# Gathered tokens of a mixture-of-experts layer: 128 partitions instead of 64, and products with identity columns instead of transposes

## The chip, the cores and the metric

The kernel runs on one core of one Trainium2 chip. The metric is the device time of one execution in microseconds (us), as the median of several runs.

## What is computed

One layer of a hybrid streaming encoder for 384 tokens (256 of a prompt, 128 of running streams) of 2048 float32 numbers each, plus 16 learned tokens ahead of the prompt. The part that the change touches is the last one, a mixture of 32 experts:

```
def hier_moe(v, w_coarse, w_fine, w_gate, w_up, w_down):
    ...
    pc = jax.nn.softmax((t @ w_coarse).astype(jnp.float32), axis=-1)
    pg, gi = lax.top_k(pc, 1)                      # one of 4 groups of 8 experts
    ...
    vals, ei = lax.top_k(lf_g, TOP_K_IN_GROUP)     # two experts in it
    ...
    hg = jnp.einsum('td,edf->tef', t, w_gate)
    hu = jnp.einsum('td,edf->tef', t, w_up)
    act = jax.nn.silu(hg) * hu * gates[:, :, None].astype(t.dtype)
    out = jnp.einsum('tef,efd->td', act, w_down)
```

Each expert has three weight matrices of 2048 x 256 (or 256 x 2048) float32 numbers, 2 MB each. With two experts for each of 384 tokens there are 768 pairs of token and expert, 24 for one expert in the mean.

## The kernel before

The first 980 us or so are the projections, the convolution, the state-space scan and the merge. Then the router runs, and then a loop over the 32 experts, on which this text concentrates. The kernel is written for each engine by hand: every engine has its own list of instructions, and semaphores order them between engines.

An expert has C = 64 slots for tokens. The router's products put into `slots` the row number of the token in each slot; an empty slot holds FAR, a number beyond all rows, and the transfer leaves such a row out. The order in which tokens take slots is a permutation (`iota_c`): the first 16 tokens of an expert go to 16 different groups of four neighbouring slots, the next 16 again.

For expert e the steps are these, by engine:

- POOL (GpSimd), `gather_e`: copies the expert's indices from `slots` to `idg`, waits until TensorE has read the tokens of the expert before, and issues one indirect DMA that brings the rows of `vbuf` in DRAM to `xg`, one slot in a partition, 8 KB each. Later `scatter_e` writes the rows of the result `yo` back to DRAM.
- PE (TensorE), `xt_`: turns `xg` (slots in partitions) into 16 blocks of 128 features by 64 slots, by 16 transposes, in two halves b of eight. `xgv` is `xg` seen as 16 interleaved blocks of columns, so that the operand that is loaded into the array has a step of 16 elements.
- ACT, `xh`, and DVE, `xl`: write each half as two rounded parts (high and low) to `xS`.
- PE, `gate_up`: 32 products of `xS` with the gate and up weights. `at_` transposes the activations, `down` makes 12 products in rounded parts for the first half of `w_down` (L1299) and four in full float32 for the second half (L1304).
- ACT, `mhi_`, and DVE, `mlo_`: split each 1 MB unit of weights into two rounded parts (`mHg`, `mLg`).
- SP, `mload`: loads the weights in units of 1 MB into nine buffers (`mraw_a` to `mraw_d`), in a fixed order, each as soon as its buffer's former unit has been split or used.

The order on PE, where the expert after next is turned while the one before is finished, is this:

```
            def body(e, c, i):
                if c > 0:
                    at_(e - 1)
                gate_up(e, c, i)
                if c < NE - 1:
                    xt_(e + 1)
                if c > 0:
                    down(e - 1, c - 1, i)
```

After the loop comes a path for experts with more than 64 tokens, which is skipped when there is none, and the final sum and norm. `CM` is 68 and `XM` is 64: in each half the first transpose has 68 rows, the other seven 64.

Of the kernel before, what the change touches and what calls it, by code (L numbers as in the profile page):

```python
# [26 lines left out]
U32 = mybir.dt.uint32  # L27
# [5 lines left out]
P = 128  # L33
# [7 lines left out]
C = 64  # L41
CM = 68
XM = 64
# [5 lines left out]
FAR = 1 << 20  # L49


def build(nc, ins, outs):
# [24 lines left out]
    NE = w_gate.shape[1]  # L77
# [15 lines left out]
    with ctx:  # L93
# [10 lines left out]
        vbuf = dram("vbuf", (T, D))  # L104
# [4 lines left out]
        ident = sb("ident", [P, P])  # L109
# [17 lines left out]
        def at(name, off, shape, dt=F32):  # L127
            n = 4
            for s in shape[1:]:
                n *= s  # L130
            assert base + off + n <= end, (name, base + off + n, end)
            return nc.alloc_sbuf_tensor_at(name, shape, dt, offset=base + off)
# [68 lines left out]
        a_k = a_w + 4 * TB + D * 4  # L201
# [20 lines left out]
        xg = at("xg", a_w + 4 * TB, [P, D])  # L222
        xgv = xg[:, :].rearrange("c (p k) -> c k p", k=KD)
# [9 lines left out]
        slots = at("slots", a_k, [P, NE, 2], U32)  # L233
        idg = at("idg", a_k + 512, [P, 2], U32)
# [19 lines left out]
        trow = at("trow", a_k + 576, [P, Q, 2], U32)  # L254
        tval = at("tval", a_k + 640, [P, Q, 2, 3], U32)
        rslots = at("rslots", a_k + 736, [P, NE])
        a_cst = a_tmp - 864
        lst = at("lst", a_cst, [P, P], BF16)
        one = at("one", a_cst + 256, [P, P], BF16)
# [20 lines left out]
        oslots = at("oslots", a_m + KD * C * 4 + 2 * C * 4 + 64, [P, NITEM, 3], U32)  # L280
# [6 lines left out]
        PS = ctx.enter_context(nc.psum_tensor("PS", [P, 8, 512], F32))  # L287
# [8 lines left out]
        pl = sem("pl")  # L296
# [37 lines left out]
        xgz = sem("xgz")  # L334
# [10 lines left out]
        sl_done = sem("sl_done")  # L345
# [7 lines left out]
        ix_done = sem("ix_done")  # L353
# [7 lines left out]
        o_w, o_ix, o_x, o_tr, o_tc, o_gu, o_si, o_am, o_at, o_ac, o_dn, o_ye, o_y = [  # L361
            sem("ovf_" + n) for n in "w ix x tr tc gu si am at ac dn ye y".split()]
# [639 lines left out]
        def _(pe):  # L1002
# [20 lines left out]
            for k in range(KD):  # L1023
# [4 lines left out]
                for q in range(Q):  # L1028
                    ins = pe.transpose(PS[:, k % 4, NM + q * P:NM + (q + 1) * P], xt[:, q, k * P:(k + 1) * P],
                                       ident[:, :])  # L1030
# [97 lines left out]
            for g in range(NH2):  # L1128
# [4 lines left out]
                for u in range(2):  # L1133
                    n = n_xb + 2 * g + u
# [8 lines left out]
            for g in range(ND2):  # L1143
                n = n_ga + 3 * g
# [28 lines left out]
            with pe.Fori(0, ND2 // 2) as i:  # L1173
                for h in range(2):
                    n, g = n_gb + 6 * i + 3 * h, 2 * i + h
# [59 lines left out]
            for r in range(Q):  # L1235
                ins = pe.matmul(PS[0:TQ, 7, (r + 1) * NE:(Q + 1) * NE], one[0:TQ, 0:TQ],
                                esum[0:TQ, r, :].unsqueeze(1).to_broadcast([TQ, Q - r, NE]), start=False,
                                stop=r == Q - 1, skip_group_check=True)
                if r < Q - 1:
                    pe.matmul(PS[0:TQ, 7, (r + 1) * NE:(r + 2) * NE], lst[0:TQ, 0:TQ], esum[0:TQ, r + 1, :],  # L1240
                              start=False, stop=True, skip_group_check=True)
# [3 lines left out]
            for m in range(2 * Q):  # L1245
                ins = pe.matmul(PS[0:C, 6, 0:2 * NE], oc[0:TQ, m // Q, m % Q, :],
                                etok[0:TQ, m // Q, m % Q].rearrange("p e v -> p (e v)"), start=m == 0, stop=m == 2 * Q - 1)
            ins.then_inc(slp_done, 1)
            pe.wait_ge(rn_done, 1)
            for m in range(2 * Q):  # L1250
                ins = pe.matmul(PS[0:C, 1, 0:NE], oc[0:TQ, m // Q, m % Q, :], erst[0:TQ, m // Q, m % Q, :],
                                start=m == 0, stop=m == 2 * Q - 1)
# [3 lines left out]
            MG = (mHg, mLg)  # L1256
            MD, AT = (mHd, mLd), (aTH, aTL)

            def xt_(e):

                pe.wait_ge(xg_in, e * 16 + 16)
                for b in range(2):
                    ge(pe, xl_done, 2 * e + b - 1)
                    for k in range(8):
                        r = XM if k else CM
                        ins = pe.transpose(PS[:, 2 + b, k * XM:k * XM + r],  # L1266
                                           xgv[0:r, 8 * b + k, :], ident[0:r, 0:r])
                    ins.then_inc(xg_tr, 1)

            def gate_up(e, c, i):  # L1270
# [61 lines left out]
            with pe.If(over > 0):  # L1332
                with pe.Fori(0, (MORE - 1) * NE) as n:
                    pe.wait_ge(o_x, n * 16 + 16)
                    for k in range(KD):
                        ins = pe.transpose(PS[:, 2 + k // 4, (k % 4) * CM:(k % 4 + 1) * CM],
                                           xgv[0:CM, k, :], ident[0:CM, 0:CM])
                    ins.then_inc(o_tr, 1)
                    pe.wait_ge(o_tc, n + 1)
                    pe.wait_ge(o_w, n * 48 + 48)  # L1340
                    for k in range(KD):
                        ins = pe.matmul(PS[0:C, 0, 0:2 * DE], oxT[:, k, :], ogu[:, :, k, :],
                                        start=k == 0, stop=k == KD - 1)
                    ins.then_inc(o_gu, 1)
                    pe.wait_ge(o_am, n + 1)
                    for k in range(2):
                        ins = pe.transpose(PS[:, 1, k * CM:(k + 1) * CM],
                                           act_[0:CM, :].rearrange("c (p k) -> c k p", k=2)[:, k, :],
                                           ident[0:CM, 0:CM])
                    ins.then_inc(o_at, 1)  # L1350
                    pe.wait_ge(o_ac, n + 1)
                    for c in range(4):
                        for k in range(2):
                            ins = pe.matmul(PS[0:C, 4 + c, :], oaT[:, k, :], odn[:, k, c * 512:(c + 1) * 512],
                                            start=k == 0, stop=k == 1)
                    ins.then_inc(o_dn, 1)
# [6 lines left out]
        def _(dve):  # L1363
# [224 lines left out]
            for c in range(2):  # L1588
                ins = dve.tensor_copy(init[:, c].rearrange("p s (m b) -> p m b s", m=2),
                                      PS[:, 7, 2 * P * c:2 * P * (c + 1)].rearrange("p (m b s) -> p m b s", m=2, s=NST))  # L1590
# [32 lines left out]
            for i in range(NH2):  # L1623
                n = n_cv + 4 * i
# [15 lines left out]
            for g in range(NH2):  # L1640
                n = n_xb + 2 * g
                lo(n + 2)
                dve.wait_ge(tap_done, g + 1)
                for kk in (1, 2):
                    for m2 in range(2):
                        t = 2 * g + m2
                        o = O_CW + kk * KH + t
                        ins = dve.scalar_tensor_tensor(out=tmp[:, m2, 0:ZW - 2], in0=zp[:, t, kk:kk + ZW - 2],
                                                       scalar=vecs[:, o:o + 1], in1=tmp[:, m2, 0:ZW - 2],
                                                       op0=ALU.mult, op1=ALU.add)  # L1650
# [6 lines left out]
                b = 2 * (g % 2)  # L1657
# [14 lines left out]
            for g in range(ND2):  # L1672
                n = n_ga + 3 * g
# [130 lines left out]
            for kk in range(2):  # L1804
# [13 lines left out]
            R(TS(efar[0:C, :], PS[0:C, 6, 0:2 * NE], 0.0, float(FAR + 1), ALU.is_equal, ALU.mult))  # L1818
            dve.scalar_tensor_tensor(out=slots[0:C, :, :].rearrange("p e v -> p (e v)"), in0=PS[0:C, 6, 0:2 * NE],
                                     scalar=-1.0, in1=efar[0:C, :], op0=ALU.add, op1=ALU.add).then_inc(sl_done, 1)  # L1820

            dve.wait_ge(slp_done, 2)
            R(dve.tensor_copy(rslots[0:C, :], PS[0:C, 1, 0:NE]))
# [131 lines left out]
        def _(pool):  # L1955
# [50 lines left out]
            pool.memset(act_[:, :], 0.0).then_inc(pad_done, 1)  # L2006
            pool.wait_ge(g_done, ND2)
            pool.memset(xg[:, :], 0.0).then_inc(xgz, 1)

            def gather(s):  # L2010
                pool.nop().then_inc(pl, 1)
                pool.indirect_dma_start(out=xg[0:C, :], out_offset=None, in_=vbuf[:, :],
                                        in_offset=bass.IndirectOffsetOnAxis(ap=idg[0:C, 0:1], axis=0),
                                        bounds_check=T - 1, oob_is_err=False).then_inc(s, 16)

            def scatter(s):
# [5 lines left out]

            def gather_e(e):
                ge(pool, xg_in, e * 16)
                pool.tensor_copy(idg[0:C, :], slots[0:C, e, :]).then_inc(ix_done, 1)  # L2025
                pool.wait_ge(ix_done, e + 1)
                ge(pool, xg_tr, e * 2)
                gather(xg_in)
# [5 lines left out]
                pool.wait_ge(yo_done, e + 1)  # L2034
                scatter(yo_out)

            pool.wait_ge(xgz, 1)
            pool.wait_ge(sl_done, 1)
            pool.wait_ge(v_out, 16 * ND2)
            gather_e(0)  # L2040

# [12 lines left out]
            with pool.If(over > 0):  # L2054
                pool.wait_ge(tab_ok, 16)
                for q in range(Q):
                    for kk in range(2):
                        pool.indirect_dma_start(
                            out=tab[:, :], out_offset=bass.IndirectOffsetOnAxis(ap=trow[0:TQ, q, kk:kk + 1], axis=0),
                            in_=tval[0:TQ, q, kk, :], in_offset=None, bounds_check=C * NITEM - 1,  # L2060
                            oob_is_err=False).then_inc(sc_out, 16)
                pool.wait_ge(osl_in, 16)
                with pool.Fori(0, (MORE - 1) * NE) as n:
                    pool.tensor_copy(idg[0:C, :], oslots[0:C, n + NE, 0:2]).then_inc(o_ix, 1)
                    pool.tensor_copy(ids[0:C, :], oslots[0:C, n + NE, 0:2]).then_inc(o_ix, 1)
                    pool.wait_ge(o_ix, n * 2 + 2)
                    gather(o_x)
                    pool.wait_ge(o_ye, n + 2)
                    scatter(o_y)
                    pool.wait_ge(o_y, n * 16 + 16)  # L2070
# [35 lines left out]
```

## Time and profile before

| | |
|---|---|
| three runs | 1606.44, 1605.02, 1602.97 us; median 1605.02 us |
| the profiled execution | 1605.18 us, of which the profile's span is 1603.4 us |
| PE busy | 1482.1 us (92% of the span) |
| DVE, ACT, POOL busy | 994.9 us (62%), 859.2 us (54%), 166.2 us (10%) |
| the expert loop | from about 1005 to 1550 us of the span |

Busy time of PE is that of matrix products as the profile models them: products that follow each other overlap, so a row's duration is longer than the distance from its start to the next one's. The distance between starts is what a product costs on PE. Loads of the stationary operand are rows of their own (PEld). "Idle" in a row is the time just before it in which its engine did nothing, with what ended that time.

### The profile page before, as it was taken

Reading aid. Unit: us, or ns where it says so; the run is one execution under the profiler, and the core shown is the slowest. Engines: PE = TensorE matmul, PEld = TensorE weight load, DVE = VectorE, ACT = ScalarE, POOL = GpSimd, SP = SyncE. Lnnn points to the kernel's source line nnn. Section 1 sums busy time; section 2 is a strip of 40 time slices with the busy share of each in tenths; the row PEclk is TensorE's granted clock in tenths of the full one; section 3 lists DMA queues with packets and bytes.
Section 4 is the critical chain, followed back from the end, with each engine's and each line's share of the span. In section 5 each row is a group of like instructions: output and inputs, shape, how many; then the busy total and the mean of one; then the engine's idle time right before and its main releaser. Section 6 shows DMA issues by size and latency. Waiting matters only on the chain.

```text
span 1603.4 us, 21338 instructions
## 1 busy us (share of the span) xinstructions
PE 1482.1 (92%) x7946; PEld 1295.8 (81%) x7946; DVE 994.9 (62%) x1253; ACT 859.2 (54%) x1073; POOL 166.2 (10%) x169
## 2 busy tenths in 40 slices
PE   3999999999999999999999996899999999999960
PEld 2999999999999999999999996676666666666630
DVE  5495777887773344332342225888887887877826
ACT  5465455565553233222242224688878778778732
POOL 0000000000000000000000001121322223222102
PEclk9999999999999999999999997899999999999985
DMA  9233433223333445444343364799999999999925
GB/s 238 61 120 115 124 102 103 90 82 115 119 108 110 127 139 196 127 130 131 123 139 115 125 224 174 267 395 393 401 396 403 400 395 403 395 383 398 392 85 226
DMA packets 160179, 343.49 MB, mean 214 GB/s; under 512 B 25446, under 2 KB 132134, under 8 KB 132200
## 3 DMA queue, kind: packets, MB, share of 16 engines
q1 hardware_dynamic: 149216, 324.82, 57.0%
q0 software_dynamic: 5632, 16.02, 3.0%
q10 hardware_dynamic: 5272, 1.84, 0.5%
q8 instruction: 39, 0.64, 0.2%
q14 instruction: 20, 0.16, 0.0%
HBM read 340.03 MB, written 23.58 MB: 227 GB/s over the span
## 4 chain that ended last, share of the span: by engine, by line
PE 68%; DMA 17%; DVE 8%; ACT 5%; issue 3%; ACTq 0%; SPq 0%; DVEq 0%; POOL 0%; POOLq 0%
PE PS L1047 49%; DMA mraw_b<-w_down 6%; PE PS L1278 6%; PE PS L1304 4%; DMA mraw_d<-w_down 4%; DMA mraw_a<-w_down 4%; DVE mLg L1828 2%; PE PS L1299 2%; ACT mHg L886 2%; DMA mraw_b<-w_up 1%; PE PS L1266 1%; PE PS L1099 1%; DVE spL L1371 1%; PE PS L1072 1%; DMA yk<-ybuf 1%
## 5 line engine op out<-in xcount | busy, mean ns | idle before, releaser
L1047 PE MATMUL PS<-uHL,spH 128*128 128x384 f32 (+2 forms) x2560 | 665.3, 341 | 3.1 <-DVE uHL L1489 1.4
L1047 PEld LDWEIGHTS PS<-uHL,spH 128*128 128x128 f32 x2560 | 464.6, 188 | 4.7 <-issue 2.5
L1371 DVE TENSOR_TENSOR spL<-raw,spH 128x2048 fp32r<-128x2048 f32 x100 | 229.0, 2291 | 340.3 <-ACT spH L633 339.1
L1047 PE MATMUL PS<-uHL,spL 128*128 128x384 f32 (+2 forms) x1280 | 433.5, 339 | 0.0
L633 ACT ACTIVATE spH<-raw 128x2048 fp32r<-128x2048 f32 x100 | 191.2, 1913 | 312.0 <-PE PS L1047 311.7
L1047 PEld LDWEIGHTS PS<-uHL,spL 128*128 128x128 f32 x1280 | 242.0, 189 | 0.0
L1278 PE MATMUL PS<-mHg,xS 128*128 128x512 f32 x512 | 207.4, 405 | 4.1 <-issue 3.9
L1278 PE MATMUL PS<-mLg,xS 128*128 128x512 f32 x512 | 203.9, 398 | 0.0
L1828 DVE TENSOR_TENSOR mLg<-mraw_b,mHg 128x2048 fp32r<-128x2048 f32 x53 | 119.7, 2289 | 35.8 <-ACT mHg L886 35.8
L1047 PE MATMUL PS<-tHL,spH 128*128 128x384 f32 x512 | 130.3, 335 | 0.0
L1278 PEld LDWEIGHTS PS<-mHg,xS 128*128 128x128 f32 x512 | 99.4, 194 | 26.9 <-issue 4.0
L1278 PEld LDWEIGHTS PS<-mLg,xS 128*128 128x128 f32 x512 | 97.9, 191 | 21.3
L1828 DVE TENSOR_TENSOR mLg<-mraw_a,mHg 128x2048 fp32r<-128x2048 f32 x43 | 97.5, 2289 | 22.4 <-ACT mHg L886 22.4
L886 ACT ACTIVATE mHg<-mraw_b 128x2048 fp32r<-128x2048 f32 x53 | 98.8, 1903 | 0.3 <-DMA mraw_b<-w_up 0.3
L1047 PEld LDWEIGHTS PS<-tHL,spH 128*128 128x128 f32 x512 | 92.5, 188 | 0.0
L1047 PE MATMUL PS<-tHL,spL 128*128 128x384 f32 x256 | 85.6, 335 | 0.0
L886 ACT ACTIVATE mHg<-mraw_a 128x2048 fp32r<-128x2048 f32 x43 | 80.5, 1901 | 0.8 <-PE PS L1278 0.8
L1266 PEld LDWEIGHTS PS<-ident,xg 64*128 64x128 f32 (+1 forms) x512 | 66.4, 199 | 16.0 <-issue 6.0
L1266 PE MATMUL PS<-ident,xg 64*128 64x64 f32 (+1 forms) x512 | 74.1, 279 | 4.0 <-DMA xg<-vbuf,idg 4.0
L908 ACT ACTIVATE yo<-PS 64x2048 f32<-64x2048 f32 x32 | 59.7, 1864 | 8.7 <-PE PS L1304 8.7
L2025 POOL COPY idg<-slots 64x2 uint32 (+1 forms) x32 | 61.8, 1932 | 21.8 <-DMA xg<-vbuf,idg 13.6
L2018 POOL DMA_INDIRECT ybuf<-yo,ids x32 | 29.7, 927 | 305.6 <-ACT yo L908 295.2
(349 smaller groups left out, 1873.2 us busy)
## 6 DMA issues: line engine op xcount, KB each, us to landing
raw<-w_in SPq DMA_DIRECT2D x64, 1024.0 KB, 5.8
mraw_b<-w_gate SPq DMA_DIRECT2D x31, 1024.0 KB
mraw_b<-w_down SPq DMA_DIRECT2D x31, 1024.0 KB
mraw_a<-w_down SPq DMA_DIRECT2D x23, 1024.0 KB
mraw_a<-w_gate SPq DMA_DIRECT2D x22, 1024.0 KB
mraw_b<-w_up SPq DMA_DIRECT2D x22, 1024.0 KB
mraw_a<-w_up SPq DMA_DIRECT2D x21, 1024.0 KB
raw<-w_o SPq DMA_DIRECT2D x16, 1024.0 KB, 5.6
```

Source lines behind the costliest of these rows:

```text
L633: act.activation(spH[:, s, :], raw[:, s, :], ACT.Copy).then_inc(hi_done, 1)
L886: act.activation(mH[s], mraw[u % MRAW], ACT.Copy).then_inc(mhi, 1)
L908: act.activation(yo[0:C, :].rearrange("p (n c) -> p n c", n=4), PS[0:C, 4:8, :], ACT.Copy).then_inc(yo_done, 1)
L1047: ins = pe.matmul(PS[:, b + m, 0:w_], PT[w][:, s, k * UW + m * P:k * UW + (m + 1) * P], rhs[:, a, k0 + k, c0:], start=first and k == 0 and ...
L1266: ins = pe.transpose(PS[:, 2 + b, k * XM:k * XM + r], xgv[0:r, 8 * b + k, :], ident[0:r, 0:r])
L1278: ins = pe.matmul(PS[:, 0, 0:2 * DE], xS[:, half * UK + k, :], MG[w][:, 2 * half:2 * half + 2, k * DE:(k + 1) * DE], start=half == 0 and k ...
L1299: pe.matmul(PS[0:CM, 4 + x, :], AT[a][:, :], MD[w][:, 0, x * 512:(x + 1) * 512], start=(w, a) == (0, 0), stop=False)
L1304: ins = pe.matmul(PS[0:CM, 4 + x, :], aTF[:, :], mraw[r][:, x * 512:(x + 1) * 512], start=False, stop=True)
L1371: dve.tensor_tensor(spL[:, s, :], raw[:, s, :], spH[:, s, :].bitcast(F32), ALU.subtract).then_inc(lo_done, 1)
L1828: TT(mL[s], mraw[u % MRAW], mH[s].bitcast(F32), ALU.subtract).then_inc(mlo, 1)
L2018: pool.indirect_dma_start(out=ybuf[:, :], out_offset=bass.IndirectOffsetOnAxis(ap=ids[0:C, 1:2], axis=0), in_=yo[0:C, :], in_offset=None, ...
L2025: pool.tensor_copy(idg[0:C, :], slots[0:C, e, :]).then_inc(ix_done, 1)
```

## The change

The 64 slots of an expert are spread over 128 partitions: slots 0 to 31 lie in partitions 0 to 31, slots 32 to 63 in partitions 64 to 95. A new table `gslots` of 128 partitions holds the indices in this layout, with FAR in the other 64 partitions; DVE fills it with two copies. The gather then names 128 rows of `xg`. On PE, each transpose of 64 (or 68) rows becomes an ordinary float32 product of all 128 rows of `xg` with 64 columns of the identity matrix (`pick`), those of the 64 used partitions. The output in PSUM is the same 64 columns in the same place.

```diff
+        gslots = at("gslots", a_k + 864, [P, NE], U32)
...
+            pick = ident[:, :].rearrange("p (a c) -> p a c", a=2)[:, :, 0:C // 2]
+
             def xt_(e):
 
                 pe.wait_ge(xg_in, e * 16 + 16)
                 for b in range(2):
                     ge(pe, xl_done, 2 * e + b - 1)
                     for k in range(8):
-                        r = XM if k else CM
-                        ins = pe.transpose(PS[:, 2 + b, k * XM:k * XM + r],
-                                           xgv[0:r, 8 * b + k, :], ident[0:r, 0:r])
+                        ins = pe.matmul(PS[:, 2 + b, k * XM:(k + 1) * XM], xgv[:, 8 * b + k, :], pick,
+                                        start=True, stop=True)
                     ins.then_inc(xg_tr, 1)
...
             dve.scalar_tensor_tensor(out=slots[0:C, :, :].rearrange("p e v -> p (e v)"), in0=PS[0:C, 6, 0:2 * NE],
                                      scalar=-1.0, in1=efar[0:C, :], op0=ALU.add, op1=ALU.add).then_inc(sl_done, 1)
+            dve.wait_ge(sl_done, 1)
+            dve.wait_ge(xgz, 2)
+            for a in range(2):
+                dve.tensor_copy(gslots[64 * a:64 * a + C // 2, :],
+                                slots[a * C // 2:(a + 1) * C // 2, :, 0]).then_inc(sl_done, 1)
...
             pool.memset(xg[:, :], 0.0).then_inc(xgz, 1)
+            pool.memset(gslots[:, :], FAR).then_inc(xgz, 1)
 
             def gather(s):
                 pool.nop().then_inc(pl, 1)
-                pool.indirect_dma_start(out=xg[0:C, :], out_offset=None, in_=vbuf[:, :],
-                                        in_offset=bass.IndirectOffsetOnAxis(ap=idg[0:C, 0:1], axis=0),
+                pool.indirect_dma_start(out=xg[:, :], out_offset=None, in_=vbuf[:, :],
+                                        in_offset=bass.IndirectOffsetOnAxis(ap=idg[:, 0:1], axis=0),
                                         bounds_check=T - 1, oob_is_err=False).then_inc(s, 16)
...
             def gather_e(e):
                 ge(pool, xg_in, e * 16)
-                pool.tensor_copy(idg[0:C, :], slots[0:C, e, :]).then_inc(ix_done, 1)
+                pool.tensor_copy(idg[:, 0:1], gslots[:, bass.ds(e, 1)]).then_inc(ix_done, 1)
...
-            pool.wait_ge(xgz, 1)
-            pool.wait_ge(sl_done, 1)
+            pool.wait_ge(xgz, 2)
+            pool.wait_ge(sl_done, 3)
```

The path for experts with more than 64 tokens is changed in the same way (products with `pick`, two index copies instead of one); the trace shows no instruction of that path.

The instructions of PE at the end of the router and at the first `xt_` of the program, before (`oc`, `etok` and `erst` are operands of the router's float32 products, `xg` the gathered tokens, `xS` their split blocks):

```order
L1246 MATMUL PS<-etok,oc 64x64 x6
L1251 MATMUL PS<-erst,oc 64x32 x6
L1266 MATMUL PS<-ident,xg 128x68
L1266 MATMUL PS<-ident,xg 128x64 x7
L1266 MATMUL PS<-ident,xg 128x68
L1266 MATMUL PS<-ident,xg 128x64 x7
L1278 MATMUL PS<-mHg,xS 128x512
```

The same place after the change:

```order
L1247 MATMUL PS<-etok,oc 64x64 x6
L1252 MATMUL PS<-erst,oc 64x32 x6
L1268 MATMUL PS<-ident,xg 128x64 x16
L1280 MATMUL PS<-mHg,xS 128x512
```

The 16 transposes became 16 products in the same place; nothing else moved on PE, there or in the loop.

The instructions of DVE at the end of the router, before (`slots` is the table of token rows, `rslots` a factor for each slot, the `mLg` rows are the first splits of weights):

```order
L1819 SCALAR_TENSOR_TENSOR slots<-PS,efar 64x64
L1823 COPY rslots<-PS 64x32
L1828 TENSOR_TENSOR mLg<-mraw_a,mHg 128x2048 x3
L1828 TENSOR_TENSOR mLg<-mraw_c,mHg 128x2048
L1832 TENSOR_TENSOR xS<-PS,xS 128x8x64 x2
```

After the change:

```order
L1821 SCALAR_TENSOR_TENSOR slots<-PS,efar 64x64
L1826 COPY gslots<-slots 32x32 x2
L1830 COPY rslots<-PS 64x32
L1835 TENSOR_TENSOR mLg<-mraw_a,mHg 128x2048 x3
L1835 TENSOR_TENSOR mLg<-mraw_c,mHg 128x2048
L1839 TENSOR_TENSOR xS<-PS,xS 128x8x64 x2
```

Two copies of 32 partitions stand between the table and the copy of `rslots`; the first gather now waits for them.

## Rows read from the trace of the kernel before

**Rows 1.** The page: busy us, share of the span, instructions of each engine.

```profile
PE 1482.1 (92%) x7946; PEld 1295.8 (81%) x7946; DVE 994.9 (62%) x1253; ACT 859.2 (54%) x1073; POOL 166.2 (10%) x169
```

**Rows 2.** Busy time by stretch: one expert early, one late in the loop.

```profile
1062.09:1078.22 16.13, 16.13 (x72) 11.03 (x70) 13.60 (x11) 13.28 (x13) 3.26 (x5) 1.00 1.01 386
1466.26:1483.52 17.26, 16.34 (x72) 10.95 (x70) 13.76 (x11) 13.35 (x13) 4.48 (x5) 1.00 1.02 394
```

**Rows 3.** Timeline of PE, the late expert: start, duration, what, idle before.

```profile
1466.26 2.31 PE L1266 MATMUL PS<-ident,xg 68*128 68x68 f32 x16
1468.49 0.45 PE L1299 MATMUL PS<-mHd,aTH 128*68 128x512 f32 x1
...
1471.05 0.39 PE L1299 MATMUL PS<-mLd,aTH 128*68 128x512 f32 x1
1472.36 3.65 PE L1304 MATMUL PS<-mraw_b,aTF 128*68 128x512 f32 x8 [0.92 <-DMA mraw_b<-w_down]
```

**Rows 4.** Waits of PE from 1150 to 1520: sum, times, longest.

```profile
PE PS L1304 <- DMA mraw_a<-w_down: 5.6, 7, 1.6
PE PS L1304 <- DMA mraw_b<-w_down: 5.6, 7, 1.0
PE PS L1304 <- DMA mraw_d<-w_down: 4.0, 6, 0.9
```

**Rows 5.** Timeline of PE: the transposes of experts 2, 9 and 31.

```profile
1029.83 2.31 PE L1266 MATMUL PS<-ident,xg 68*128 68x68 f32 x16
...
1142.72 2.31 PE L1266 MATMUL PS<-ident,xg 68*128 68x68 f32 x16
...
1517.83 2.31 PE L1266 MATMUL PS<-ident,xg 68*128 68x68 f32 x16
...
1523.72 0.65 PE L1304 MATMUL PS<-mraw_b,aTF 128*68 128x512 f32 x1 [0.69 <-DMA mraw_b<-w_down]
```

**Rows 6.** Operand loads of three lines: count, duration min/median/max in ns.

```profile
L1266 PEld LDWEIGHTS PS<-ident,xg x512: 182/202/205, 998.9 to 1519.8; 64*128 64x128 f32 x149, 68*128 68x128 f32 x22
...
L1246 PEld LDWEIGHTS PS<-etok,oc x12: 182/227/227, 991.7 to 992.8; 128*64 128x64 f32 x12
...
L1194 PEld LDWEIGHTS PS<-wr,hT x96: 190/192/192, 846.9 to 982.0; 128*128 128x128 f32 x96
```

**Rows 7.** Timeline of operand loads (PEld): four series of float32 loads.

```profile
153.48 1.93 PEld L1072 LDWEIGHTS PS<-u,We 128*128 128x128 f32 x16
...
846.92 1.42 PEld L1194 LDWEIGHTS PS<-wr,hT 128*128 128x128 f32 x12
...
991.71 1.35 PEld L1246 LDWEIGHTS PS<-etok,oc 128*64 128x64 f32 x12 [1.84 <-DVE oc L1807]
...
1466.41 2.02 PEld L1266 LDWEIGHTS PS<-ident,xg 64*128 64x128 f32 x15 [0.19 <-issue]
```

**Rows 8.** Stretch from the first transposes to the first expert's products, as Rows 2.

```profile
998.86:1005.35 6.49, 2.62 (x17) 2.11 (x17) 6.46 (x6) 2.48 (x3) 3.36 (x2) 0.50 0.90 317
```

**Rows 9.** Timeline of POOL and DVE at the router's end.

```profile
993.90 0.18 POOL L2025 COPY idg<-slots 64x2 uint32<-64x2 uint32 x1 [8.13 <-DVE slots L1819]
994.93 0.18 DVE L1823 COPY rslots<-PS 64x32 f32<-64x32 f32 x1 [1.17 <-PE PS L1251]
```

**Rows 10.** POOL in the late expert; gathers from 1150 to 1520, issue to landing.

```profile
1469.44 0.96 POOL L2012 DMA_INDIRECT xg<-vbuf,idg  x1 [2.37 <-PE PS L1266]
...
DMA to landing us min/median/max: 7.2/7.7/8.5
```

**Rows 11.** DMA packets in two stretches: 1183.5 to 1186 (a gather), 1180 to 1183.

```profile
DMA packets 152, 0.75 MB, mean 302 GB/s; under 512 B 60, under 2 KB 60, under 8 KB 60
...
DMA packets 172, 1.25 MB, mean 418 GB/s; under 512 B 19, under 2 KB 19, under 8 KB 19
```

**Rows 12.** Chain that ended last, in order of time, in the late expert.

```profile
1466.97 2.29 DVE mLg L1828
...
1469.28 20.14 DMA mraw_d<-w_down
```

More of the change, by code:

```diff
@@ L1335, in _ @@
                     for k in range(KD):
-                        ins = pe.transpose(PS[:, 2 + k // 4, (k % 4) * CM:(k % 4 + 1) * CM],
-                                           xgv[0:CM, k, :], ident[0:CM, 0:CM])
+                        ins = pe.matmul(PS[:, 2 + k // 4, (k % 4) * CM:(k % 4) * CM + C], xgv[:, k, :], pick,
+                                        start=True, stop=True)
                     ins.then_inc(o_tr, 1)
@@ L2063, in _ @@
                 with pool.Fori(0, (MORE - 1) * NE) as n:
-                    pool.tensor_copy(idg[0:C, :], oslots[0:C, n + NE, 0:2]).then_inc(o_ix, 1)
+                    for a in range(2):
+                        pool.tensor_copy(idg[64 * a:64 * a + C // 2, :],
+                                         oslots[a * C // 2:(a + 1) * C // 2, n + NE, 0:2]).then_inc(o_ix, 1)
+                        pool.wait_ge(o_ix, n * 3 + a + 1)
+                        pool.nop().then_inc(pl, 1)
                     pool.tensor_copy(ids[0:C, :], oslots[0:C, n + NE, 0:2]).then_inc(o_ix, 1)
-                    pool.wait_ge(o_ix, n * 2 + 2)
+                    pool.wait_ge(o_ix, n * 3 + 3)
                     gather(o_x)
```

## The prediction

> **What bounds the kernel now.** I first read the page's busy times: PE is busy for 92% of the span, the next engine, DVE, for 62% [rows 1]. PE comes first, then, but such a share mixes stages. The change lies in the expert loop alone, so I read two single experts by stretch, each from the start of its transposes to the start of the next expert's [rows 2]. The early one takes 16.13 us and PE is busy for all 16.13: there PE is the bound, and 16.13 us is what an expert costs when PE waits for nothing. The late one takes 17.26 us, of which PE is busy for 16.34, while the DMA engines are full (share 1.02): there something else ends last. The timeline of PE names it: the products of L1304, which use the second half of w_down, start 1.31 us after the start of the product before them (1472.36 - 1471.05), having stood idle for 0.92 us until that transfer landed [rows 3]. The waits of PE from 1150 to 1520 are all of this one kind, 20 of them with 15.2 us of idle time [rows 4]. In the chain that ended last the link ahead of such a product is a w_down transfer of 20.14 us, issued when a split freed its buffer [rows 12]. So the loop has two phases: PE sets the pace at first while DMA falls behind its lead, and from about 1145 DMA sets it.
>
> How much that costs in all: expert 2's transposes start at 1029.83 and expert 31's at 1517.83, 29 experts in 488.0 us [rows 5]. At 16.13 us each they would take 467.8 us, so 20.2 us are lost to DMA. The first seven of these (to 1142.72) take 112.9 us, which is 7 x 16.13: no loss there. The other 22 take 375.1 us, 17.05 us each. That is the DMA's pace, and the 20.2 us are slack on PE: work added there is free until it has filled the wait.
>
> **The price of the products.** The transposes' operand loads are 512 records, 16 for each of 32 experts: one record for one transpose [rows 6]. The router's L1246 is an ordinary float32 product; the program's list of PE has six, the trace 12 loads [rows 6]. An ordinary float32 product is thus two loads and two passes where a transpose is one of each. The change therefore makes 32 records of 16 in each expert.
>
> What does one cost? The moving side is short (64 columns), so the load of the 128 x 128 operand sets the pace. Twelve such loads of L1194 take 1.42 us, the last one 0.19 by itself: (1.42 - 0.19) / 11 = 0.112 us from one to the next [rows 6, 7]. Sixteen of L1072 give (1.93 - 0.19) / 15 = 0.116. The gathered block is read with a step of 16 elements, which I don't know of these two; the transposes of now, which read it so, come to (2.02 - 0.20) / 14 = 0.130 with the changes between 68 and 64 rows in it, and that is my upper bound. The lower is L1246 with (1.35 - 0.23) / 11 = 0.102 [rows 6, 7], of the same two-pass kind, though with 64 columns loaded. I take 0.112, since L1194's loads are float32 and have the new operand's shape.
>
> So the new transposition takes 32 x 0.112 = 3.58 us; the old takes 1468.49 - 1466.26 = 2.23 us [rows 3]. PE gains 1.35 us of work for each expert; the bounds are 3.26 - 2.23 = 1.03 and 4.16 - 2.23 = 1.93. The 16 loads of only 64 rows save nothing that could be given back, since the record count decides. The Trainium skill (FP8 and Floating Point Precision, TensorE Precision Notes) says that true float32 takes four passes through the array; the two loads of each L1246 product don't agree with four loads, and by four the sum would be that of the last rival below.
>
> **What hides it.** PE's expert becomes 16.13 + 1.35 = 17.48 us, above the DMA's 17.05. PE is then the bound all through the loop, and the wait at L1304 goes to nothing: w_down lands when it did, and PE comes later. For 29 experts that is 29 x 17.48 = 506.9 against 488.0, or +18.9 us. Expert 31's transposition adds 1.35 more, and the 0.69 us of idle time ahead of the L1304 behind it go [rows 5]: +0.7.
>
> **The start.** The first transposition runs at half the clock (granted 0.50, the level of 1.2 GHz) in a stretch where DVE is busy for 6.46 of 6.49 us with the first splits [rows 8]. Sixteen records more there cost between nothing (DVE's splits hide it) and some 3 us; expert 1's, right behind, lies partly beside the chain through ACT and DVE to the first activations. I take +1 us, with 0 to 3 as bounds.
>
> **The gather.** The same rows of 8 KB move. Its longer index list may cost POOL more than the 0.96 us of now, but the rows land 7.2 to 8.5 us after the issue at 1469.44, and are wanted at 1483.52: some 6 us of cover [rows 10, 2]. Were they later than that, PE would wait for xg. PE reads xg 1.35 us longer, so the next gather starts that much later, inside the same cover. The two copies of DVE at the router's end (0.18 us each, as the row L1823) stand in DVE's 1.17 us of idle time ahead of L1823; POOL's first index copy at 993.90 moves back by about 0.4 us [rows 9], which is part of the 1 us above. Behind a waiting L1823 stand the first splits; they don't move.
>
> What the layout does to DMA can be bounded. While a gather's rows land, the core moves 302 GB/s; just before, 418 [rows 11]. If the 2.5 us ran at the full rate, DMA would gain 2.5 x (1 - 302/418) = 0.69 us for each expert. The Trainium skill (SBUF — State Buffer, Door 1: The DMA port swizzle) says that partitions 0 to 63 reach only 8 of 16 ports, and 64 to 127 the others; the dip in the row is of the kind that this would cause, and by the rule it would go. It is what speaks most for the change. But a DMA pace of 16.4 us changes nothing when PE needs 17.48, so I count nothing for it, and nothing for a dip that stays.
>
> **The sum.** 18.9 + 0.7 + 1 = 20.6 us on the profiled execution's own 1605.18 us: 1625.8, say 1626 us. That execution is 0.16 us from the median of the three runs, so the same number stands for the median. With the lower price: 29 x 1.03 - 20.2 = 9.7, and 1.03 - 0.69 = 0.3: 1615. With the upper: 29 x 1.93 - 20.2 = 35.8, and 1.93 - 0.69 = 1.2, and 3: 1645.
>
> **Rivals.**
>
> *Faster.* A product with the identity is one record, as a transpose is. Then the block costs 16 x 0.112 = 1.8 us, PE's expert is 15.7, DMA is the bound in nearly all of the loop, and if the dip goes, 22 experts save 0.69 us each: 15 us, 1590 us. For it speaks the dip; against it the 12 records of L1246 for six products. The point from which it decides is the block's growth: below 20.2 / 29 = 0.70 us for an expert the whole is not slower, that is under 2.93 us for the block or 0.092 us for each of 32 records. No row is that low.
>
> *Same.* One record, and the dip stays: DMA goes on at 17.05 us, 1605 us.
>
> *Much slower, the wait stays.* The loads are issued when a split frees a buffer, and splits follow PE: if a slower PE makes w_down later by as much, nothing is absorbed and all is added: 30 x 1.35 + 1 = 41.5, 1647 us. A gather that loads some of the DMA engines twice would do the same. Against it: in the first seven experts PE set the pace with the same buffers and never waited [rows 5].
>
> *Much slower, four loads.* If a product of this shape took four loads and not two, the block would take 64 x 0.112 = 7.17 us: 30 x (7.17 - 2.23) - 20.2 + 1 = 129, 1734 us. The two records of L1246 speak against it.
>
> **How the numbers follow.** The forecast has 0.82, the wait that stays 0.07, four loads 0.02, one record with the dip gone 0.06, one record without 0.03. The predicted time is the forecast's, 1626 us; the range is its two bounds, 1615 to 1645 us. The runs before lie within 3.5 us, and 0.2% is 3.2 us, about what can be told from no change. Slower by more: 0.82 + 0.07 + 0.02 = 0.91; faster 0.06; same 0.03.
>
> **What would show it.** In the changed kernel's trace: 1024 records of the product on xg, 0.112 us apart, and about 3.6 us from its first to the next product; experts of about 17.5 us through the whole loop, early ones too; PE busy all the time in late experts, with hardly any wait of L1304 for w_down; a DMA share in the loop below 1. I am wrong if the count is 512, if the early experts still take 16.1 us, or if the waits at L1304 stay beside longer blocks.

## The result, and the profile after

The changed kernel takes 1773.72 us (median of four runs, 1772.71 to 1775.36) against 1605.6 us: a ratio of 1.105, 95% interval 1.104 to 1.107. The forecast was 1626 us, range 1615 to 1645. The direction was right, the size was off by 148 us.

The page's line of busy times, which answers to [rows 1]:

```profile
PE 1668.0 (94%) x8458; PEld 1477.0 (83%) x8458; DVE 1001.1 (56%) x1255; ACT 858.9 (48%) x1073; POOL 173.8 (10%) x170
```

PE has 512 records more and 186 us more of busy time (1668.0 against 1482.1), while the other engines do about what they did. The same experts by stretch, which answers to [rows 2]; here two neighbouring experts are cut at the start of the block on `xg`, at the first product of `down` behind it, and at the first full float32 product (columns: stretch and its length, then busy us and records of PE, PEld, DVE, ACT, POOL, then the granted clock, the DMA share and GB/s):

```profile
1194.95:1201.70 6.75, 6.75 (x33) 6.75 (x33) 4.67 (x5) 1.86 (x4) 0.83 (x1) 0.91 0.92 352
1201.70:1205.50 3.80, 3.80 (x15) 2.19 (x15) 1.78 (x2) 3.52 (x3) 1.23 (x2) 0.71 0.58 216
1205.50:1216.59 11.09, 11.09 (x43) 7.47 (x42) 7.48 (x5) 7.96 (x7) 2.50 (x2) 1.00 0.84 304
1216.59:1223.34 6.75, 6.75 (x33) 6.75 (x33) 4.62 (x5) 1.80 (x4) 0.78 (x1) 0.83 0.93 347
1223.34:1228.20 4.86, 4.86 (x15) 2.70 (x14) 2.84 (x2) 4.19 (x3) 1.23 (x2) 0.54 0.54 202
```

Three things are to be seen. The block takes 6.75 us, where the forecast had 3.58. In the twelve products behind it the clock is granted at 0.71 and 0.54 in the mean, and they take 3.80 and 4.86 us. And DMA, full before at a share of 1.01 to 1.02, has room: PE is busy without a gap, and from 1040 to 1680 its list of waits is empty. The w_down waits of [rows 4] are gone, as forecast.

The operand loads of the block: the line's own view (count, duration min/median/max), and the same loads in the timeline, which answer to [rows 6] and [rows 7]:

```profile
L1268 PEld LDWEIGHTS PS<-ident,xg x1024: 290/311/313, 1002.6 to 1689.5; 128*128 128x128 f32 x171
```

```profile
1194.71 7.04 PEld L1268 LDWEIGHTS PS<-ident,xg 128*128 128x128 f32 x32
```

There are 1024 records, 32 for each expert: two for each product, as forecast. But a load lasts 0.311 us and not 0.19, and the loads start (7.04 - 0.31) / 31 = 0.217 us apart and not 0.112. The timeline of PE behind the block shows the clock product by product (start, duration):

```profile
1194.95 7.00 PE L1268 MATMUL PS<-ident,xg 128*128 128x64 f32 x32
1201.70 0.68 PE L1301 MATMUL PS<-mHd,aTH 128*68 128x512 f32 x1
1202.18 0.63 PE L1301 MATMUL PS<-mHd,aTL 128*68 128x512 f32 x1
...
1204.36 0.39 PE L1301 MATMUL PS<-mHd,aTL 128*68 128x512 f32 x1
```

A product of 512 columns lasts 0.63 us just behind the block and 0.39 us from about 1204 on: the 1.2 GHz level, and then 2.4 GHz again.

Where the 170.2 us between the two profiled spans (1773.6 and 1603.4) lie, follows from the blocks of experts 2 and 31, as in [rows 5]:

```profile
1038.88 7.00 PE L1268 MATMUL PS<-ident,xg 128*128 128x64 f32 x32
...
1683.04 7.00 PE L1268 MATMUL PS<-ident,xg 128*128 128x64 f32 x32
```

Up to expert 2 it is 1038.88 - 1029.83 = 9.05 us; from there to expert 31 it is 644.16 - 488.0 = 156.2 us, 22.21 us for an expert; behind it 5.0 us, about the growth of one more block (6.75 - 2.23 = 4.52 us).

The start, on POOL and PE, which answers to [rows 5] and [rows 9]:

```profile
993.80 0.18 POOL L2033 COPY idg<-gslots 128x1 uint32<-128x1 uint32 x1 [8.54 <-DVE gslots L1826]
994.96 2.97 POOL L2020 DMA_INDIRECT xg<-vbuf,idg  x1 [0.98 <-POOL idg L2033]
```

```profile
1002.61 7.20 PE L1268 MATMUL PS<-ident,xg 128*128 128x64 f32 x32 [8.24 <-DMA xg<-vbuf,idg]
1011.27 0.76 PE L1280 MATMUL PS<-mHg,xS 128*128 128x512 f32 x1 [1.46 <-issue]
```

The first gather is issued at the old time, but its rows are there at 1002.61 and no longer at 998.86 [rows 8]: 3.75 us later. The expert's first product follows at 1011.27 instead of 1005.35, 5.9 us later.

### The profile page after: what moved, and what is told of

Read it like the earlier page. It is cut to its first block, busy times and chain, and to the rows that moved or that the text cites. A ratio compares the mean times of both kernels' runs of the same rounds, so it can differ in the third digit from the quotient of the medians.

```text
span 1773.6 us, 22395 instructions
## 1 busy us (share of the span) xinstructions
PE 1668.0 (94%) x8458; PEld 1477.0 (83%) x8458; DVE 1001.1 (56%) x1255; ACT 858.9 (48%) x1073; POOL 173.8 (10%) x170
## 4 chain that ended last, share of the span: by engine, by line
PE 90%; DVE 5%; ACT 2%; DMA 2%; issue 1%; ACTq 0%; SPq 0%; POOL 0%; POOLq 0%; DVEq 0%
PE PS L1048 45%; PE PS L1280 14%; PE PS L1268 12%; PE PS L1301 8%; PE PS L1306 6%; PE PS L1100 1%; DVE spL L1373 1%; DMA yk<-ybuf 1%; PE PS L1073 1%; ACT ys L676 1%; PE PS L1219 1%; PE PS L1195 1%; PE PS L1030 1%; DMA ldrow<-log_dt 1%; DVE htok L1948 1%
## 5 line engine op out<-in xcount | busy, mean ns | idle before, releaser
L1268 PEld LDWEIGHTS PS<-ident,xg 128*128 128x128 f32 x1024 | 225.2, 310 | 9.7 <-DMA xg<-vbuf,idg 8.4
L1268 PE MATMUL PS<-ident,xg 128*128 128x64 f32 x1024 | 224.0, 389 | 8.2 <-DMA xg<-vbuf,idg 8.2
L892 ACT ACTIVATE xS<-PS 128x512 fp32r<-128x512 f32 x64 | 38.2, 597 | 174.9 <-PE PS L1268 174.9
L1839 DVE TENSOR_TENSOR xS<-PS,xS 128x512 fp32r<-128x512 f32 x64 | 44.3, 692 | 99.2 <-ACT xS L892 99.2
L1301 PE MATMUL PS<-mHd,aTH 128*68 128x512 f32 x128 | 73.5, 574 | 4.6 <-DVE mLd L1835 4.6
```

The lines of the kernel that those rows point to most:

```text
L892: act.activation(xS[:, 8 * b:8 * b + 8, 0:XM], PS[:, 2 + b, :].rearrange("p (k c) -> p k c", k=8), ACT.Copy).then_inc(xh_done, 1)
L1268: ins = pe.matmul(PS[:, 2 + b, k * XM:(k + 1) * XM], xgv[:, 8 * b + k, :], pick, start=True, stop=True)
L1301: pe.matmul(PS[0:CM, 4 + x, :], AT[a][:, :], MD[w][:, 0, x * 512:(x + 1) * 512], start=(w, a) == (0, 0), stop=False)
L1839: TT(xS[:, 8 * b:8 * b + 8, XM:], PS[:, 2 + b, :].rearrange("p (k c) -> p k c", k=8), xS[:, 8 * b:8 * b + 8, 0:XM].bitcast(F32), ALU.subtr ...
```

## The experiments

Three theories on why a record takes twice the price were told apart. **A**: a plain product's load is slow when its operand is read with a step (the 128 columns of a block stand 16 elements apart). **B**: it is slow because 128 rows are read so, not 64. **C**: it is the moving operand, which is now two pieces of 32 columns.

### Steps, rows, pieces

Run `e3_contiguous_load` changes one line; features come in another order, which changes the values:

```diff
-        xgv = xg[:, :].rearrange("c (p k) -> c k p", k=KD)
+        xgv = xg[:, :].rearrange("c (k p) -> c k p", k=KD)
```

> As the changed kernel, but the loaded block is 128 neighbouring columns of the token rows and no longer every 16th; the features so go to other rows of the products, which changes the values and nothing of the work. Theories A and B: records 0.112 us apart, a block of 3.6 us, which is the price of the forecast: 1620 to 1630 us if the wait for w_down absorbs what the forecast said and the clock stays up, some 45 us more if the clock falls behind the block as before. Theory C (two pieces of the moving operand): still 0.217 and 1770 to 1775 us.

Measured: 1627.22 us, ratio 1.014 (1.012 to 1.016). The line's loads, the block in the timelines of PE and PEld, and an expert by stretch:

```profile
L1268 PEld LDWEIGHTS PS<-ident,xg x1024: 187/192/333, 1002.0 to 1542.8; 128*128 128x128 f32 x171
```

```profile
1191.35 3.77 PEld L1268 LDWEIGHTS PS<-ident,xg 128*128 128x128 f32 x32
```

```profile
1191.58 3.68 PE L1268 MATMUL PS<-ident,xg 128*128 128x64 f32 x32
1195.07 0.43 PE L1301 MATMUL PS<-mHd,aTH 128*68 128x512 f32 x1
...
1197.89 0.59 PE L1306 MATMUL PS<-mraw_d,aTF 128*68 128x512 f32 x1
```

```profile
1191.58:1209.00 17.42, 17.42 (x88) 12.62 (x87) 13.63 (x11) 13.22 (x13) 4.53 (x5) 1.00 0.97 375
```

The same 32 records now take 3.49 us (1195.07 - 1191.58), an expert 17.42 us, the clock stays at 1.00, and the 12 products behind the block take 2.82 us (1197.89 - 1195.07). The forecast had 3.58, 17.48 and 1626: with the step gone, its working of the loop holds (of the start it does not, as is told below).

Run `e4_one_piece_moving` gives the moving operand in one piece (partitions 32 to 63, which are empty, in place of slots 32 to 63):

```diff
-                        ins = pe.matmul(PS[:, 2 + b, k * XM:(k + 1) * XM], xgv[:, 8 * b + k, :], pick,
+                        ins = pe.matmul(PS[:, 2 + b, k * XM:(k + 1) * XM], xgv[:, 8 * b + k, :], ident[:, 0:C],
```

> As the changed kernel, but the moving operand is the first 64 columns of the identity in one piece, so that partitions 32 to 63 (empty rows) stand where slots 32 to 63 should, which changes the values and nothing of the work. Theories A and B: still 0.217 us for a record, 1770 to 1775 us. Theory C: 0.112 us, a block of 3.6 us, 1620 to 1630 us.

Measured: 1775.31 us (one run), loads of 0.310 us in the median. C falls.

Run `e2_products_64` keeps the layout of before and changes only the operation:

```diff
-                        ins = pe.transpose(PS[:, 2 + b, k * XM:k * XM + r],
-                                           xgv[0:r, 8 * b + k, :], ident[0:r, 0:r])
+                        ins = pe.matmul(PS[:, 2 + b, k * XM:(k + 1) * XM], xgv[0:XM, 8 * b + k, :],
+                                        ident[0:XM, 0:XM], start=True, stop=True)
```

> The layout of before (64 slots in 64 partitions), only the 16 transposes become plain products of 64 rows with the 64 x 64 identity. Theory A (plain product with a step in its loaded operand): 32 records 0.217 us apart, a block of 6.8 us, 1765 to 1775 us. Theory B (128 rows at a step): 32 records at 0.112, a block of 3.6 us, 1620 to 1630 us, as the forecast had it. Theory C (the moving operand's two pieces of 32 columns): also 3.6 us and 1620 to 1630 us.

Measured: 1812.14 us, ratio 1.129 (1.127 to 1.131). The loads, and two experts by stretch:

```profile
L1265 PEld LDWEIGHTS PS<-ident,xg x1024: 288/307/310, 998.3 to 1723.9; 64*128 64x128 f32 x171
```

```profile
1200.11:1223.17 23.06, 23.06 (x87) 16.89 (x86) 13.96 (x11) 13.38 (x13) 4.41 (x5) 0.85 0.83 307
1223.17:1246.58 23.41, 23.41 (x88) 17.10 (x87) 13.83 (x11) 13.25 (x13) 4.24 (x5) 0.85 0.67 243
```

B falls: 64 rows are as dear as 128. Theory A had 1765 to 1775, so 37 us more need a reason. The block is 7.13 us, 0.38 more than in the changed kernel, and the 1.2 GHz level lasts longer: 6.8 to 10.2 us for an expert and not 3.4 or 6.8, so that the 12 products of `down` take up to 5.18 us. The operation alone is thus the whole loss; the layout gives a part of it back.

### How large a step

Run `e6_steps_2_to_16` loads products 1 to 4 of a block with a step of 2 elements, the next with 4, 8 and 16 (`blk` gives the columns; they aren't the right features).

```diff
+            def blk(n):
+                st = (2, 4, 8, 16)[n // 4]
+                return xg[:, :].rearrange("c (a p k) -> c a k p", p=P, k=st)[:, 0, n % 4 if st > 2 else n % 2, :]
...
-                        ins = pe.matmul(PS[:, 2 + b, k * XM:(k + 1) * XM], xgv[:, 8 * b + k, :], pick,
+                        ins = pe.matmul(PS[:, 2 + b, k * XM:(k + 1) * XM], blk(8 * b + k), pick,
```

> As the changed kernel, but the 16 products of a block load columns with a step of 2 elements (products 1 to 4), 4 (5 to 8), 8 (9 to 12) and 16 (13 to 16), which mixes the features up and changes nothing of the work. If there is one bound between cheap and dear, records are 0.112 or 0.217 us apart and nothing between; with the bound between 8 and 16 elements the block is 24 x 0.112 + 8 x 0.217 = 4.4 us and the time about 1655 us, with it between 4 and 8 the block is 5.3 us and the time 1680 us or more. If the price grows with the step, there are four different distances.

Measured: 1768.52 us (one run). The records start 0.118, 0.233, 0.238 and 0.217 us apart with steps of 2, 4, 8 and 16 (medians over the loop): both places that I had named for the bound were wrong; it lies between 2 and 4. Run `e10_steps_2_3_4_15` puts steps of 2, 3, 4 and 15 on lines of their own, in this way:

```diff
+                    for k in range(4, 8):
+                        if b == 0:
+                            ins = pe.matmul(PS[:, 2 + b, k * XM:(k + 1) * XM], xg[:, k % 2:k % 2 + 382:3], pick,
+                                            start=True, stop=True)
```

> As the changed kernel, but the products of a block load columns with a step of 2 elements (1 to 4), 3 (5 to 8), 4 (9 to 12) and 15 (13 to 16), each four on a line of their own, which mixes the features up and changes nothing of the work. The run with steps 2, 4, 8 and 16 gave about 0.118, 0.233, 0.238 and 0.217 us for a record. Theory S (a plain product's load is slow from a size of step on): 15 is as dear as 16, and step 3 falls on one of the two sides; a block of 5.6 us with step 3 cheap, 6.5 us with it dear, and 1720 to 1770 us. Theory Z (steps of a power of two are dear): steps 3 and 15 take 0.118 us, the block 4.7 us, and 1660 to 1670 us.

Measured: 1750.31 us (one run). The timeline of operand loads in one block, with steps of 2, 3, 4 and 15 from top to bottom:

```profile
1229.21 1.13 PEld L1269 LDWEIGHTS PS<-ident,xg 128*128 128x128 f32 x8
1230.26 1.47 PEld L1273 LDWEIGHTS PS<-ident,xg 128*128 128x128 f32 x8
1231.65 1.95 PEld L1277 LDWEIGHTS PS<-ident,xg 128*128 128x128 f32 x8
1233.50 1.94 PEld L1281 LDWEIGHTS PS<-ident,xg 128*128 128x128 f32 x8
```

Eight loads take 1.13, 1.47, 1.95 and 1.94 us; the records within each eight start 0.118, 0.174, 0.233 and 0.230 us apart (medians over the loop). Theory Z falls, since 15 is as dear as 16. Theory S holds only in part: there is no single bound; the price rises by half at 3, doubles at 4, and stays there. The Trainium skill (Advanced Engine Details and Errata, SBUF Cachelines) says that SBUF has lines of 16 bytes, and that it takes at least two hits on a line to run at full speed. Such a line holds four float32 numbers, so that a step of 2 at most is free. An estimate from the page's figure is that four elements in a row lie on two lines at a step of 2, on three at 3 and on four from 4 on, so that the prices should be as 1, 1.5, 2 and 2, and the four measured prices agree with it. They agree for plain products only: the transposes of before, with a step of 16, started 0.110 us apart, and those of L1189 in the same trace, on neighbouring columns, 0.109. Why a transpose is spared, no run here shows.

### The clock

Run `e7_contiguous_twice` is `e3_contiguous_load` with every product of the block issued twice:

```diff
-                    for k in range(8):
+                    for k in [x // 2 for x in range(16)]:
```

> The run with neighbouring columns loaded (1627 us, block 3.49 us, clock at its full level throughout the loop), with each product of a block issued twice: 64 records, 7.0 us, as long as the changed kernel's block of slow loads (6.75 us), but with twice as many records in it. Theory T (TensorE's clock falls behind a stretch of that length without long products): the clock falls to 0.50 behind the blocks as in the changed kernel, an expert takes 20.9 + 1.5 = 22.4 us and the run about 1780 us. Theory R (it falls since few records run in that time): the clock stays at 1.00, 20.9 us for an expert, 1627 + 31 x 3.5 = 1735 us.

Measured: 1745.5 us (one run). The block's loads, and one expert by stretch:

```profile
1191.47 7.34 PEld L1268 LDWEIGHTS PS<-ident,xg 128*128 128x128 f32 x64
```

```profile
1191.70:1212.66 20.96, 20.96 (x119) 16.17 (x118) 13.84 (x11) 13.33 (x13) 4.55 (x5) 1.00 0.84 323
```

Theory R: a block as long as the changed kernel's, but of 64 quick records, leaves the clock at 1.00. So the fall belongs to the stretch of slow loads and not to its length without long products. What the chip goes by in it, these runs don't tell.

Run `e9_products_interleaved` moves the changed kernel's products between the long ones of `gate_up`:

```diff
+                            if half and c < NE - 1:
+                                xt_one(e + 1, 2 * k + w)
...
                 gate_up(e, c, i)
-                if c < NE - 1:
-                    xt_(e + 1)
```

> The changed kernel with its 16 plain products of a block no longer in a row but one behind each of the 16 products of 512 columns of gate_up's second half; nothing else differs. Theory H (the load path is the bound while slow loads run, and they overlap the products ahead of them): a pair takes two slow loads and one of 0.112 us, 0.55 us, 16 pairs 8.7 us instead of 3.8 + 6.75 = 10.5; the clock then stays at 1.00 (no stretch of slow loads alone), an expert takes 22.2 - 1.8 - 1.5 = 18.9 us and the run about 1675 us. Theory N (a slow load overlaps nothing): a pair takes 0.23 + 0.43 = 0.66 us, 16 pairs 10.6 us as now; only the clock's 1.5 us are won, 20.7 us, about 1727 us. If the clock still falls, 1.5 us more for an expert in either.

Measured: 1684.3 us (one run). The timeline of PE, and the stretch of the 16 pairs:

```profile
1188.35 0.44 PE L1266 MATMUL PS<-ident,xg 128*128 128x64 f32 x2
1188.60 0.48 PE L1286 MATMUL PS<-mLg,xS 128*128 128x512 f32 x1
1188.92 0.43 PE L1266 MATMUL PS<-ident,xg 128*128 128x64 f32 x2
```

```profile
1188.35:1197.40 9.05, 9.05 (x50) 8.95 (x50) 5.18 (x3) 4.07 (x4) 3.28 (x2) 1.00 1.01 410
```

Theory H: a pair takes 0.57 us (1188.92 - 1188.35), with PEld busy for 8.95 of 9.05 us; an expert takes 19.11 us (18.9 was expected). The clock stays up. So the slow load occupies the load path, and only a part of it hides.

### Transposes in the new layout

Run `e1_transposes_128` keeps the layout and goes back to transposes, for 14 of the 16 blocks; each writes 64 columns too many, which the next overwrites:

```diff
+            perm = ident[:, :].rearrange("p (a h c) -> p h a c", a=2, h=2)
...
+                        if k < 7:
+                            ins = pe.transpose(PS[:, 2 + b, k * XM:(k + 2) * XM], xgv[:, 8 * b + k, :], perm)
+                        else:
+                            ins = pe.matmul(PS[:, 2 + b, k * XM:(k + 1) * XM], xgv[:, 8 * b + k, :], pick,
+                                            start=True, stop=True)
```

> The layout over 128 partitions stays; of the 16 products of a block 14 become transposes of all 128 rows and 128 columns, whose 64 unused output columns the next one overwrites; the last of each half stays a plain product. Theory A (the plain product's step of 16 elements in its loaded operand makes a load 0.217 us; a transpose reads the same step at 0.11): the block is 14 x 0.11 + 4 x 0.217 = 2.4 us, PE's expert about 16.3 us, and the time 1590 us (gather's dip gone) to 1610 us (dip stays). Theory B (128 rows read at a step are slow, whatever the kind): 14 x 0.217 + 0.87 = 3.9 us for the block, an expert of 17.8 us, some 1635 us. In both the clock's fall behind the block, if it comes from the block's length, is rarer or gone; if it stays as it was, some 45 us more.

Measured: 1587.53 us, ratio 0.989 (0.987 to 0.991), faster than both kernels. The block in the timeline of PE, an expert by stretch, and the DMA packets in the 2.5 us of a gather, as in [rows 11]:

```profile
1192.79 0.94 PE L1271 MATMUL PS<-ident,xg 128*128 128x128 f32 x7
1193.57 0.54 PE L1273 MATMUL PS<-ident,xg 128*128 128x64 f32 x2
1193.95 0.99 PE L1271 MATMUL PS<-ident,xg 128*128 128x128 f32 x7
1194.78 0.54 PE L1273 MATMUL PS<-ident,xg 128*128 128x64 f32 x2
1195.12 0.43 PE L1306 MATMUL PS<-mHd,aTH 128*68 128x512 f32 x1
```

```profile
1192.79:1209.00 16.21, 16.21 (x74) 11.46 (x72) 13.68 (x11) 13.37 (x13) 4.76 (x5) 1.00 1.01 409
```

```profile
DMA packets 242, 1.05 MB, mean 420 GB/s; under 512 B 114, under 2 KB 114, under 8 KB 114
```

Seven transposes of 128 rows take 0.78 us (1193.57 - 1192.79) at a step of 16: theory A again. The block is 2.33 us, 0.1 more than before, and yet the kernel is 18 us faster: every expert takes 16.21 us, with no wait for w_down. The gather's dip is gone, 420 GB/s against 302 [rows 11].

Run `e5_list128_partitions64` keeps that and puts the slots back into partitions 0 to 63, with the same list of 128 indices:

```diff
-                dve.tensor_copy(gslots[64 * a:64 * a + C // 2, :],
+                dve.tensor_copy(gslots[32 * a:32 * a + C // 2, :],
```

> As the run with 14 transposes and 2 plain products in a block (1587.5 us, 16.21 us for an expert), with the same list of 128 indices, but the 64 slots in partitions 0 to 63 and the empty ones in 64 to 127. Theory P (the partitions in which the rows land made the gather's dip): DMA falls to about 300 GB/s for 2.5 us after each gather again, w_down is waited for, late experts take about 17 us, 1603 to 1607 us. Theory L (the list or the transposes' form took the dip away): no waits, 16.21 us for an expert, 1587 us.

Measured: 1597.62 us, ratio 0.996 (0.994 to 0.997): between the two theories. The packets in 2.5 us of a gather, at the same distance from its issue, and the waits of PE from 1150 to 1490 (sum, times, longest):

```profile
DMA packets 246, 1.05 MB, mean 420 GB/s; under 512 B 118, under 2 KB 118, under 8 KB 118
```

```profile
PE PS L1311 <- DMA mraw_a<-w_down: 2.8, 3, 1.3
PE PS L1311 <- DMA mraw_b<-w_down: 2.3, 4, 0.8
PE PS L1311 <- DMA mraw_d<-w_down: 1.6, 4, 0.7
```

That dip goes with the list of 128, in either place. But the late experts are no faster for it: the waits for w_down come back, 6.7 us here, only later than the kernel before had them, and from 1307.69 on 12 experts take 204.68 / 12 = 17.06 us each, as before (17.05). This is their line by stretch:

```profile
1307.69:1512.37 204.68, 197.25 (x865) 136.61 (x864) 164.28 (x121) 159.50 (x145) 50.69 (x48) 1.00 1.00 397
```

As differences between runs, the list, with the longer transposes that came with it, is worth some 8 of the 18 us, and the place of the rows the other 10. That it is the lost dip that gives the 8 is not shown, and what the transfers do otherwise to cost the 10 was not found.

Run `e8_interleaved` puts the 14 transposes and 2 products between `gate_up`'s, with the edit of `e9_products_interleaved`:

```diff
+                            if half and c < NE - 1:
+                                xt_one(e + 1, 2 * k + w)
```

> The run with 14 transposes and 2 plain products (1587.5 us), with each of a block's 16 products behind one of the 16 products of 512 columns of gate_up's second half instead of all behind the last. If a transpose's load then hides beside the 512-column product ahead of it, a product on the tokens costs only its columns: PE gains something between 0 and 2.3 us for an expert (0.11 us for each of 16 is 1.8 us now). The DMA share is 1.01 already, so that the wait for w_down comes back if PE gets much below 16.2 us: between 1560 us (DMA's pace 0.8 us lower than PE's of now) and 1587 us (DMA's pace is 16.2). If taking turns costs PE more than the block did, slower than 1587 us.

Measured: 1583.89 us, ratio 0.987 (0.986 to 0.989), the lowest of all, though its interval overlaps that of `e1_transposes_128`. The timeline of PE, and 335 us of the loop by stretch:

```profile
1188.25 0.27 PE L1269 MATMUL PS<-ident,xg 128*128 128x128 f32 x1
1188.28 0.48 PE L1292 MATMUL PS<-mLg,xS 128*128 128x512 f32 x1
1188.60 0.27 PE L1269 MATMUL PS<-ident,xg 128*128 128x128 f32 x1
```

```profile
1155.00:1490.00 335.00, 335.00 (x1504) 244.28 (x1503) 283.50 (x209) 276.71 (x252) 93.69 (x84) 1.00 1.01 415
```

A pair takes 0.35 us, where a long product alone took 0.23: the transpose's 0.11 does not hide in it. An expert takes 16.06 us instead of 16.21. PE is still busy throughout, but this doesn't say that DMA keeps that pace: transfers of w_down take longer and longer from issue to landing (last column, us), here from 1040 to 1120 and from 1400 to 1490:

```profile
mraw_a<-w_down SPq DMA_DIRECT2D x3, 1024.0 KB, 7.6
mraw_a<-w_down SPq DMA_DIRECT2D x4, 1024.0 KB, 13.2
```

DMA falls behind slowly, and the loop ends before its lead is used up.

## Why the prediction was wrong

**Records.** Right: 1024 records, two for a product. Not four: the rival with 64 loads came nearest in time (1734 us), but by another way. That two records cost two of the usual distances does not hold for long products: with 512 columns each of the eight records of L1304 takes (3.65 - 0.59) / 7 = 0.44 us [rows 3], a product in rounded parts 0.23. Here, with 64 columns, the load is longer and sets the price.

**The price of a record.** This is the step that failed. The forecast priced it at 0.112 us from L1194 and bounded it above by 0.130, from the transposes, "which read it so". It saw the step of 16 elements and looked for its cost in the only rows that had it; but a transpose doesn't show that cost and a plain product does. The measured price is 0.217, the block 6.75 us and not 3.58, the growth for an expert 4.52 us (6.75 - 2.23) and not 1.35, far beyond the upper bound of 1.93. With the step taken away the block is 3.49 and the kernel takes 1627.22 us.

**What hides it.** Right: the waits are gone and the slack of 20.2 us is used up. With the measured growth the forecast's own sum gives 29 x 4.52 - 20.2 = 110.9 of the loop's 156.2 us.

**The clock.** Left out, without a reason. The forecast reckoned with the 1.2 GHz level at the start and took 2.4 GHz for granted in the loop. The 12 products behind the block take 3.80 and 4.86 us in turn instead of 2.82, in the mean 1.5 us for an expert, 44 us in 29. With the 110.9 that makes 155 of 156.2.

**The start.** 9.05 us, where the forecast had 1 and at most 3. It expected POOL's first index copy 0.4 us later; the copy stands where it stood, but the first gather's landing came 3.75 us later. The first issue, with 128 indices, holds POOL for 2.97 us where that of 64 held it for 1.09, which is 1.9 of it. The number of indices alone does not explain this: the second issue took 2.55 us before, with 64, and 1.04 after, with 128, and from 1150 on an issue takes about 1.0 us in both. The other part was not followed. With neighbouring columns this term is still 5.2 us, as expert 2 shows in that run (1035.04), and there a loop of 504.5 us instead of the forecast's 506.9 makes up for a part of it.

**The gather.** Counted at nothing, and nothing it was, since PE sets the pace after. But the layout has a gain: it is in the 18 us of `e1_transposes_128`. Its 1587.5 us come near the forecast's *faster* rival (1590 us), and, as there, most of the block is of one record each and the dip is gone. The path is another, though: the rival had PE's expert at 15.7 us and DMA as the bound, and here PE is the bound all through with 16.21, so that the nearness is in part luck. The rule of the Trainium skill that was cited there (SBUF — State Buffer, Door 1: The DMA port swizzle) does not by itself account for that dip: in `e5_list128_partitions64` all rows land in partitions 0 to 63, and the row shows no dip. It may bear on the 10 us that the place is worth, which no run here shows.

## What to carry to other kernels

Price an operation from a row with the same operation and the same access pattern: a row that shares the shape, and another that shares the step, don't make a bound together. At the full clock, plain float32 products want a loaded operand whose elements stand at most two apart; a transpose took a step of 16 at no cost. And where a new stretch changes what TensorE does, price the products behind it at 1.2 GHz too, as one end of the range.

## What was not expected

The slow load does not depend on TensorE's clock. In the changed kernel's first block, at 1.2 GHz, the 32 loads take 7.01 us, and 7.04 us in the loop, mostly at 2.4 GHz; with neighbouring columns they take 6.90 us and 3.77 us. The first blocks of the changed kernel and of `e3_contiguous_load` by stretch (the records of the block alone: PE, PEld, granted clock, DMA share, GB/s):

```profile
1002.61:1009.81 7.20, 7.20 (x32) 7.01 (x32) 0.50 0.95 382
```

```profile
1001.96:1009.05 7.09, 7.09 (x32) 6.90 (x32) 0.50 0.97 387
```

At the low clock the step costs next to nothing (7.01 against 6.90 us); at the high one the slow load stays at its price of the low.
